# Middle chunks of the dense feed-forward by 128 inner columns for all tokens, and six probability buffers

## What is computed

```python
D_MODEL, SEQ, D_FF = 1024, 256, 2816

def swiglu(x, w_gate, w_up, w_down):
    return (jax.nn.silu(x @ w_gate) * (x @ w_up)) @ w_down

# attention, with 16 heads of 64 in ab and c, and 4 heads of 256 in mem
s = jnp.einsum('bhqd,bhkd->bhqk', q, k) * scale   # plus a bias in c, a window and a sink in b
p = jax.nn.softmax(s, axis=-1)
o = jnp.einsum('bhqk,bhkd->bhqd', p, v)
```

## Time and profile before

| | |
|---|---|
| runs | 2688.63, 2691.82, 2692.26 us, median 2691.82 |
| the profiled execution | 2692.51 us, span 2691.3 us |
| TensorE (PE) busy | 2575.4 us, 96% |
| weight loads (PEld) | 1747.7 us, 65% |
| VectorE (DVE) | 1056.7 us, 39% |
| ScalarE (ACT) | 817.7 us, 30% |
| GpSimd (POOL) | 176.1 us, 7% |
| DMA | 641 MB, mean 238 GB/s |
| mean granted TensorE clock | 0.981 of 2.4 GHz |

### The profile page before, as it was taken

The page is one execution under the profiler, slowest core; times in us unless marked ns, Lnnn a source line. Parts: engine busy times, 40 slices in busy tenths (PEclk is TensorE's granted clock), DMA queues, the critical chain, the costliest instruction groups (busy, mean ns, idle before and its releaser), DMA issues.

```text
span 2691.3 us, 37633 instructions
## 1 busy us (share of the span) xinstructions
PE 2575.4 (96%) x16619; PEld 1747.7 (65%) x16619; DVE 1056.7 (39%) x1458; ACT 817.7 (30%) x1127; POOL 176.1 (7%) x178
## 2 busy tenths in 40 slices
PE   7999998999999999999998998899999998899998
PEld 5788776444444444444447886787887887688886
DVE  4655553010101011010106457736456444655544
ACT  4343342010101001010114435544344433544432
POOL 1200120000000000000000002000000004500000
PEclk9999998999999999999998999999999999899999
DMA  7555447999999999999985544345546547254651
GB/s 246 176 188 188 138 168 290 359 346 368 374 363 374 364 376 363 374 351 362 374 301 172 179 137 141 123 159 202 189 156 204 180 163 201 82 193 152 218 179 57
DMA packets 336507, 641.27 MB, mean 238 GB/s; under 512 B 16084, under 2 KB 128768, under 8 KB 336336
## 3 DMA queue, kind: packets, MB, share of 16 engines
q1 hardware_dynamic: 329840, 618.59, 64.7%
q0 software_dynamic: 6496, 20.20, 2.6%
HBM read 637.68 MB, written 1.05 MB: 237 GB/s over the span
## 4 chain that ended last, share of the span: by engine, by line
PE 89%; DVE 5%; ACT 2%; POOL 2%; DMA 1%; issue 1%; SPq 0%; ACTq 0%; DVEq 0%
PE bank L558 16%; PE bank L559 16%; PE bank L560 16%; PE bank L1081 15%; PE bank L1095 7%; PE bank L1128 7%; PE bank L1149 4%; DVE part_lo L533 2%; PE bank L877 1%; PE bank L1113 1%; PE bank L906 1%; PE bank L1057 1%; PE bank L729 1%; PE bank L570 1%; POOL bias L2153 1%; DMA raw<-in_w_in_dram 1%
## 5 line engine op out<-in xcount | busy, mean ns | idle before, releaser
L533 DVE TENSOR_TENSOR part_lo<-raw,part_hi 128x2048 fp32r<-128x2048 f32 x251 | 576.9, 2305 | 298.7 <-ACT part_hi L525 298.2
L525 ACT ACTIVATE part_hi<-raw 128x2048 fp32r<-128x2048 f32 x251 | 477.3, 1911 | 37.0 <-DMA raw<-in_c_w_in_dram 19.5
L558 PE MATMUL bank<-part_hi,x_hi 128*128 128x512 f32 x1088 | 445.3, 409 | 17.9 <-DVE part_lo L533 14.2
L559 PE MATMUL bank<-part_lo,x_hi 128*128 128x512 f32 x1088 | 438.3, 403 | 0.0
L560 PE MATMUL bank<-part_hi,x_lo 128*128 128x512 f32 x1088 | 432.0, 397 | 0.0
L558 PEld LDWEIGHTS bank<-part_hi,x_hi 128*128 128x128 f32 x1088 | 207.4, 191 | 67.4 <-DVE part_lo L533 20.5
L560 PEld LDWEIGHTS bank<-part_hi,x_lo 128*128 128x128 f32 x1088 | 207.4, 191 | 50.7
L559 PEld LDWEIGHTS bank<-part_lo,x_hi 128*128 128x128 f32 x1088 | 208.0, 191 | 43.8
L1081 PE MATMUL bank<-raw,expert_in 128*64 128x512 f32 x896 | 215.8, 603 | 2.5 <-ACT expert_in L1214 2.5
L1081 PE MATMUL bank<-raw_hi,expert_in 128*64 128x512 f32 x896 | 212.2, 594 | 0.0
L2121 DVE SCALAR_TENSOR_TENSOR h<-silu,slot_gate,bank 128x256 f32<-128x256 f32 x56 | 26.9, 480 | 462.3 <-ACT silu L1565 462.3
(11 more groups left out here) (268 smaller groups left out, 3476.4 us busy)
## 6 DMA issues: line engine op xcount, KB each, us to landing
raw<-in_exp_w_gate_dram SPq DMA_DIRECT2D x112, 512.0 KB, 6.6
raw<-in_exp_w_up_dram SPq DMA_DIRECT2D x112, 512.0 KB, 7.5
raw_hi<-in_exp_w_gate_dram SPq DMA_DIRECT2D x112, 512.0 KB, 8.4
raw_hi<-in_exp_w_up_dram SPq DMA_DIRECT2D x112, 512.0 KB, 9.2
raw<-in_exp_w_down_dram SPq DMA_DIRECT2D x56, 1024.0 KB, 12.8
raw_hi<-in_exp_w_down_dram SPq DMA_DIRECT2D x56, 1024.0 KB, 14.1
raw<-in_ffn_w_gate_dram SPq DMA_DIRECT2D x110, 512.0 KB, 4.0
raw<-in_ffn_w_up_dram SPq DMA_DIRECT2D x110, 512.0 KB, 5.2
```

Source lines behind the costliest of these rows:

```text
L525: p.nc.scalar.activation(p.part_hi[i][:, :], p.raw[i][:, :], ACT.Copy).then_inc(*self.rounded.step((name,)))
L533: p.nc.vector.tensor_tensor(p.part_lo[i][:, :], p.raw[i][:, :], p.part_hi[i][:, :].bitcast(F32), ALU.subtract).then_inc(*self.split.step(( ...
L558: nc.tensor.matmul(out, stat_hi, move_hi, start=start, stop=False, skip_group_check=True)
L559: nc.tensor.matmul(out, stat_hi, move_lo, start=False, stop=False, skip_group_check=True)
```

## The change

Four things.

1. The chunks 2 to 8 of the dense stages ("middle") are no longer cut by token tiles but by tiles j of 128 inner columns, for all 256 tokens (`pe_tile_up`, `pe_tile_down`). The weights are stationary in the up part, and x moves, as in `pe_transposed`; the gate goes to the first 256 columns of the bank, up to the second. The hidden values come out with the inner columns on the partitions, which is how the down part wants them, so the middle chunks have no transposes. The down part does both token tiles with one tile of the down weights' rows. The first two and last two chunks stay as they were.
2. In the middle chunks ScalarE and VectorE make the high and low parts straight from `h` in SBUF, and the early split stands behind them.
3. The attentions have six probability buffers (`PROB`) in place of four.
4. In the c stage two of VectorE's eight subtractions ahead of the attention move behind the first pair's bias addition.

```diff
+PROB = 6
...
 def ffn_order():
...
-    middle = [(q, tt) for q in range(2, n - 2) for tt in range(TT)]
+    middle = [(q, j) for q in range(2, n - 2) for j in range(2)]
...
+def by_tiles(q):
+    return 2 <= q < NFF - 2
...
+def pe_tile_up(p, st, k, q, j, kh):
+    slot = (st, "up", q, kh)
+    w_hi, w_lo = p.ring.ready(slot)
+    for tt in range(TT):
+        p.pe.wait_ge(*p.v.at("x", st, 2 * tt + kh))
+    for m in range(2):
+        for k4 in range(4):
+            kk = kh * 4 + k4
+            w = slice(k4 * 512 + m * FC + j * P, k4 * 512 + m * FC + (j + 1) * P)
+            mm = product(p.nc, p.bank[4 + k % 2][:, m * T:(m + 1) * T], w_hi[:, w], w_lo[:, w],
+                         p.x_hi[:, kk, :], p.x_lo[:, kk, :], start=(kk == 0 and m == 0), stop=(kk == KT - 1))
...
+def pe_tile_down(p, st, k, q, j):
+    slot = (st, "down", q)
+    w_hi, w_lo = p.ring.ready(slot)
+    p.pe.wait_ge(*p.v.at("hT", st, k))
+    for tt in range(TT):
+        for half in range(2):
+            cols = slice(j * D + half * 512, j * D + (half + 1) * 512)
+            mm = product(p.nc, p.bank[2 * tt + half][:, :], p.hT_hi[k % 2][:, tt, :], p.hT_lo[k % 2][:, tt, :],
+                         w_hi[:, cols], w_lo[:, cols])
...
 def pe_ffn(p, st):
...
-        if k:
+        if k and not by_tiles(order[k - 1][0]):
             pe_ffn_turn(p, st, k - 1)
...
 def act_ffn(p, st):
...
-        p.ring.round(*early)
-        act.wait_ge(*p.t.at("h_turned", st, k))
         if k >= 2:
             act.wait_ge(*p.t.at("down", st, k - 2))
+        if by_tiles(q):
+            act.wait_ge(*p.v.at("h", st, k))
+            act_high_and(p, p.hT_hi[k % 2][:, :, :], p.h[k % 2][:, :].rearrange("p (j t) -> p j t", j=2), "hT_hi", st, k)
+            p.ring.round(*early)
...
 def dve_ffn(p, st):
...
+        hidden = p.h[k % 2][:, :] if by_tiles(q) else p.bank[6 + k % 2][:, 0:FC]
+        dve_low(p, p.hT_lo[k % 2][:, :, :], hidden.rearrange("p (j t) -> p j t", j=2), p.hT_hi[k % 2][:, :, :], "hT", st, k)
+        if by_tiles(q):
+            p.ring.subtract(*early)
...
 def dve_attention(p, st, heads, items, scale, prob, cat_hi, cat_lo, meanwhile):
...
-            if i >= 4:
-                dve.wait_ge(*p.t.at("p_turned", st, i - 4))
+            if i >= PROB:
+                dve.wait_ge(*p.t.at("p_turned", st, i - PROB))
...
 def dve_c(p, st):
...
-    p.ring.subtract(*slots[4:12])
-    dve_attention(p, st, c_heads(p, st), PAIRS, HD ** -0.5, [g[f"p{i}"] for i in range(4)], g["cat_hi"], g["cat_lo"],
-                  {1: lambda: p.ring.subtract(slots[12]), 3: lambda: p.ring.subtract(slots[13]),
+    p.ring.subtract(*slots[4:10])
+    dve_attention(p, st, c_heads(p, st), PAIRS, HD ** -0.5, p.prob(g), g["cat_hi"], g["cat_lo"],
+                  {0: lambda: p.ring.subtract(slots[10], slots[11]), 1: lambda: p.ring.subtract(slots[12]), 3: lambda: p.ring.subtract(slots[13]),
```

More of the change, by code:

```diff
@@ L760, in pe_ffn @@
             pe_turn_rows(p, st - 1, 1)
-        pe_ffn_up(p, st, k, q, tt, 1)
+        up(p, st, k, q, part, 1)
         if k:
-            pe_ffn_down(p, st, k - 1, *order[k - 1])
+            down = pe_tile_down if by_tiles(order[k - 1][0]) else pe_ffn_down
+            down(p, st, k - 1, *order[k - 1])
     k = len(order) - 1
@@ L995, in pe_c @@
     }
[L996 removed]
+    pe_attention(p, st, c_heads(p, st), PAIRS, p.prob(g), [g["pT0"], g["pT1"]], meanwhile)
     pe_out_projection(p, st, 12, g["cat_hi"], g["cat_lo"], early=True)
@@ L1669, in dve_ffn @@
         early, late = dense_splits(p, st, k)
-        p.ring.subtract(*early)
+        if not by_tiles(q):
+            p.ring.subtract(*early)
         if k == last - 1:
```

60 lines of the change are left out of this document (39 added, 21 removed).

## The result

| | before | the change |
|---|---|---|
| median of the runs on one chip | 2692.04 us (2688.63 to 2692.83, 4 runs) | 2671.30 us (2670.87 to 2671.43, 4 runs) |
| the profiled execution, and its span | 2692.51, 2691.3 | 2671.43, 2669.9 |
| mean granted TensorE clock | 0.981 | 0.985 |

The ratio is 0.9929, with a 95% interval of 0.9916 to 0.9941: faster by 0.7%. The forecast was 2674.5 us, in a range of 2665 to 2685.

What follows compares the result with a forecast made beforehand. TensorE, busy for 2575 of 2691.3 us, was taken to bound the kernel. 9.5 (dense) + 3.4 (ab) + 4.5 (c) = 17.4 us off 2692.5 gave 2675.1, on the median 2674.5 us, range 2665 to 2685.

Steps and rivals of the forecast that it cites:

- A middle chunk before: Dense stages: an old chunk takes 8.60 us, 5.83 up and 2.77 down, with 0.24 for transposes and what they disturb.
- A middle chunk after: Dense stages: 48 steps of 0.1187 us make 5.70 for 5.83, 0.135 a chunk, 9.5 us over 70 chunks.
- The hand-over at nothing: Middle chunks: high and low parts made from SBUF, splits behind them, cost nothing, covered by over 2 us of slack.
- Six buffers in ab, 3.4 us: ab attention: VectorE no longer waits for TensorE's transposes and its own work bounds the rounds; 3.4 us, bounds 1.5 and 4.5.
- Rival A: Attentions give nothing while the dense part holds, since a circle can close again over ScalarE: 2682.5 us, chance 0.13.
- the forecast's own sign of being wrong: Attentions: a new wait, for pT or for the bias, of the size of the old one.
- Six buffers in c at nothing: c attention: transposed half projections fill TensorE between rounds, so VectorE's waits have nothing behind them; zero gain.
- Two subtractions moved, 4.5 us: c attention: second scores start 5.0 us earlier, third at 2296 to 2297.5 against 2301.97; 4.5 us, bounds 2 and 6.5.
- the bound of 6.5: c attention: upper bound in us for moving the subtractions, if the shorter gap also ends the low clock sooner.
- Rival B: Dense part gives almost nothing, by a step of 0.1209 or more or costly form changes: 2682 to 2684 us, chance 0.12.
- rival C: Dense stages: weight load binds, step 0.19 us for 0.12, so the kernel gets slower, 2914 us; chance 0.03.
- Rival D: More than forecast: a step of 0.1174 and the clock's short drops in the attentions vanish, 2667 us; chance 0.10.

Runs made afterwards that it cites:

- no_turn: The change with middle chunks in the old 512-column form, their transposes left out so the hidden values stay unturned: 2666.76 us, ratio 0.9912 to the kernel before.
- order_back: The change with each middle chunk's early split put back ahead of the high and low parts: 2672.66 us, ratio 0.9930 to the kernel before.
- prob_only: The kernel before with six probability buffers alone: 2690.09 us, ratio 0.9998 to the kernel before.
- ab_late: The change with ab's last two blocks' rounding and subtractions moved from rounds 4 to 6 to rounds 8 and 10: 2667.07 us, ratio 0.9908.
- ab_fill: The change with identity transposes added on TensorE in two waits of ab, 12 and 20: 2668.82 us, ratio 0.9919 to the kernel before.
- subs_only: The kernel before with the two subtractions of c moved alone: 2685.06 us, ratio 0.9979 to the kernel before.
- tiles_only: The change with its new middle chunks alone, four probability buffers and c's subtractions where they were: 2678.82 us, ratio 0.9956 to the kernel before.

## Why the prediction was right, and where not

- **The forecast as a whole** (2674.5, measured 2671.3) holds, and its sum of 17.4 us stands against 17.9 in the pieces with an edit. Two of its three terms were too small and one was wrong, and they cancel: that the sums agree is luck. The further 3 us came from pieces that no edit touches; with the pieces alone the time would be 2674.
- **A middle chunk before**: 0.24 us for "the transposes with what they disturb". no_turn confirms it, 0.24.
- **A middle chunk after**: mis-sized. The step of 0.1187 and the 5.70 us of the up part are exact. The term was 0.135 us a chunk and measured 0.167. I left the down part at its old price, 2.77, and it takes 2.74. That makes 11.8 us for 9.5.
- **The hand-over at nothing**: right, by the timeline (6.5 us of slack) and by order_back.
- **Six buffers in ab, 3.4 us**: this step failed; ab and mem took 0.3 us more in one execution of the change and 1.0 less in the other. The size of the waits was right: TensorE is idle for 3.2 us less between the first scores and the last projection. What failed is that a shorter wait was counted as a shorter time, with the clock at nothing: the same matmuls took 3.5 us more, at 0.84 for 0.90, with 0.50 behind the waits of 1.9 and 3.0 us. The rounds went otherwise than forecast too. The forecast put the last pair's bias additions, of which 1698.26 is the first, 3.5 us earlier, since "VectorE's own work bounds the rounds"; counted from the first scores they start 1.6 us earlier (1688.58 from 1651.20, 1698.26 from 1659.31). What it left out was ScalarE's list, where the split of round 5 stands ahead of the exponentials and these ahead of the next `pT`, and VectorE's own split in round 4. I had added up VectorE's work over the attention, and not asked round by round what TensorE gets next. Rival A named it ("ScalarE also has its exponentials, copies and high parts in each round, and a circle can close again over it") and was given 0.13 for both attentions together; and the forecast's own sign of being wrong, a new wait for `pT` of the size of the old one, is there with 3.04 us. prob_only shows the gain missing without the other edits, ab_late the part of the splits and ab_fill the part of the clock.
- **Six buffers in c at nothing**: no contradiction. prob_only took 2.2 us less there, twice the spread of that piece, but beside the moved subtractions they change nothing.
- **Two subtractions moved, 4.5 us**: right in its mechanism, mis-sized. The second scores come 5.5 us earlier against the first (forecast 5.0), since the first scores ran partly at the full clock (1.35 us for 2.08), and the low clock that followed lasted half as long. Measured 5.4 alone (subs_only), 5.3 and 6.4 in the change; the bound of 6.5 was taken for just this. The second bias pair at 2280.37 and GpSimd's bias at 2281.36 were in time for the third scores, as forecast. The wait was 1.91 us, in the forecast's 1.5 to 2.
- **Rival B** (a step of 0.1209, or a price for the change of form) and **rival C** (the load binds): not seen. The step is 0.1187 with loads listed longer than that, and the stage shows no gap. The Trainium skill's rule that stood beside rival C ("TensorE: Matmul & The Clock Gate", section "Back-to-back issue gap"), from which the change was estimated to lose about 100 us, doesn't agree with the trace of the change either: 0.1187 a step at 256 columns and 0.2283 at 512.
- **Rival D** (a step of 0.1174, and the clock's drops vanish): neither came. In ab the time at 0.50 grew; only in c it shrank.

## What to carry to other kernels

Price a new form by a stretch of the same form in the same kernel, and price also what it takes away with it: here the transposes were the whole gain, and the form a fee. A buffer that opens a circle pays only if nothing else stands in the rounds that it shortens, so go through every engine's list round by round, and move what isn't urgent out of it in the same edit, to a round whose first wait is early. A wait that is taken away is time gained only if the granted clock stays where it was, so look at the clock behind the waits that are left.

## What the runs showed of the hardware that I had not expected

- A wait of TensorE can cost more than its length. In ab of the change a wait of 1.93 us and one of 3.04 were each followed by a stretch at 0.50 of the clock, where eight score matmuls take 2.08 us and not 1.13. With the same waits filled with transposes the clock stayed at 1.00. It isn't every wait: before, one of 2.43 us in this attention had 1.00 behind it, and the same wait in tiles_only had this:

```profile
1681.50:1684.00 2.50, 2.50 (x12) 1.57 (x8) 0.63 (x4) 0.60 (x1) 0.00 (x0) 0.50 0.00 0
```

- Twelve matmuls of 512 columns in the down part take 2.74 us behind a run of 256-column matmuls and 2.77 behind one of 512, 0.2283 and 0.2308 a step, with the same operands. Why is open.
- Pieces without an edit differ by up to 6 us (1252.9 to 1259.1) between executions of kernels that are alike there, and by 0.1 us in a dense stage. Pieces with waits carry the scatter, and the time at the low clock in them goes with it: from the first dense stage to the second it was 33.8 to 33.9 us in the four executions that took 1116.0 to 1116.5, and 44.0 to 47.6 in the nine that took 1119.4 to 1120.7.
